# LayerNorm of a convolution branch: sums added first, the variance with tokens on partitions, the root on 128x4

## The reference

```python
def _layernorm(x, g, b):
    mu = jnp.mean(x32, axis=-1, keepdims=True)
    xc = x32 - mu
    y = xc * lax.rsqrt(jnp.mean(xc * xc, axis=-1, keepdims=True) + LN_EPS)
    return y * g + b

def _conv_module(u, ...):
    a, gt = u[..., :C_CONV], u[..., C_CONV:]
    h = a * jax.nn.sigmoid(gt)
    h = conv_general_dilated(h, conv_w, ...) + conv_b      # depthwise, width 31
    h = jax.nn.silu(_layernorm(h, ln_g, ln_b))
    return h @ w_pw_out
...
g = jax.nn.sigmoid(u_g + b_gate)
merged = g[..., :D] * y_conv + g[..., D:] * y_attn
```

## Time and profile before

| what | us |
|---|---|
| median of 3 runs | 3293.29 (3289.09 to 3296.37) |
| span of the profiled execution | 3293.2 |
| TensorE busy in it | 3180.6 |
| VectorE busy in it | 2023.7 |
| ScalarE busy in it | 1300.5 |
| GpSimd busy in it | 790.1 |

### The profile page before, as it was taken

How to read it: one execution, slowest core, us unless ns; L and a number is a source line. 1 busy time by engine, 2 the same in 40 slices (tenths; PEclk the granted TensorE clock), 3 DMA queues, 4 the chain that set the end, 5 groups by cost and what they waited for, 6 DMA issues and landing times.

```text
span 3293.2 us, 41912 instructions
## 1 busy us (share of the span) xinstructions
PE 3180.6 (97%) x15077; PEld 2620.5 (80%) x15077; DVE 2023.7 (61%) x3433; ACT 1300.5 (39%) x2213; POOL 790.1 (24%) x674
## 2 busy tenths in 40 slices
PE   8987999999999999999999999999999999999998
PEld 7865788788888888778887878876888888788886
DVE  6997357688807447599895862759667588510001
ACT  4336421533237431351112854228675168420111
POOL 3432200065775100011313520000212325101212
PEclk9998999999999999999999999999999999999999
DMA  7973856599893656535555046552555520445554
GB/s 236 302 242 128 307 188 208 185 292 289 290 298 122 243 202 216 195 139 194 192 192 185 14 182 226 206 180 90 217 192 193 201 74 20 173 166 193 194 196 165
DMA packets 178529, 635.97 MB, mean 193 GB/s; under 512 B 11358, under 2 KB 96906, under 8 KB 116777
## 3 DMA queue, kind: packets, MB, share of 16 engines
q1 hardware_dynamic: 164016, 583.05, 51.0%
q10 hardware_dynamic: 14328, 50.42, 3.9%
HBM read 474.04 MB, written 159.38 MB: 192 GB/s over the span
## 4 chain that ended last, share of the span: by engine, by line
PE 78%; ACT 5%; issue 3%; DVE 3%; DMA 1%; POOL 0%; ACTq 0%; DVEq 0%; POOLq 0%; SPq 0%
PE PS L1862 19%; PE PS L1813 15%; PE PS L1815 15%; PE PS L1814 15%; PE PS L2033 3%; PE PS L1836 2%; PE PS L1837 1%; PE PS L1838 1%; ACT TMP L903 1%; PE PS L2055 1%; PE PS L2056 1%; ACT probs L1028 1%; DVE W L1405 1%; PE PS L2086 1%; PE PS L2087 1%
## 5 line engine op out<-in xcount | busy, mean ns | idle before, releaser
L1862 PE MATMUL PS<-WS,HT 128*128 128x512 f32 x2088 | 482.7, 391 | 3.3 <-POOL WS L571 3.3
L1862 PEld LDWEIGHTS PS<-WS,HT 128*128 128x128 f32 x2088 | 393.9, 189 | 85.8 <-issue 3.7
L704 POOL TENSOR_TENSOR TMP<-TMP 128x512 f32<-128x512 f32 x88 | 114.5, 1302 | 1294.6 <-ACT TMP L1153 1294.6
L571 POOL TENSOR_TENSOR WS<-RAW,WS 128x1024 fp32r<-128x1024 f32 x116 | 279.9, 2413 | 569.1 <-ACT WS L776 556.3
L1813 PE MATMUL PS<-HF,WS 128*128 128x512 f32 x1024 | 398.7, 389 | 1.3 <-ACT TMP L903 0.9
L1815 PE MATMUL PS<-HF,WS 128*128 128x512 f32 x1024 | 398.4, 389 | 0.0
L1814 PE MATMUL PS<-HF,WS 128*128 128x512 f32 x1024 | 398.4, 389 | 0.0
L1422 DVE TENSOR_SCALAR_CACHE_REDUCE flags<-W,cand 128x640 uint8<-128x640 f32 (+9 forms) x272 | 372.6, 1370 | 35.6 <-DVE cand L1457 27.8
L1813 PE MATMUL PS<-HT,WS 128*128 128x512 f32 x816 | 322.2, 395 | 0.3 <-DVE HT L1242 0.3
L1815 PE MATMUL PS<-HT,WS 128*128 128x512 f32 x816 | 317.8, 389 | 0.0
L1814 PE MATMUL PS<-HT,WS 128*128 128x512 f32 x816 | 317.5, 389 | 0.0
(11 more groups left out here) (287 smaller groups left out, 6417.0 us busy)
## 6 DMA issues: line engine op xcount, KB each, us to landing
WS<-split_weights_scratch SPq DMA_DIRECT2D x234, 1024.0 KB, 4.8
split_weights_scratch<-WS SPq DMA_DIRECT2D x116, 1024.0 KB, 5.0
W<-split_weights_scratch SPq DMA_DIRECT2D x114, 1024.0 KB, 4.8
RAW<-in_w_in SPq DMA_DIRECT2D x34, 512.0 KB, 6.1
RAW<-in_w_ffn_gate SPq DMA_DIRECT2D x22, 512.0 KB, 6.3
RAW<-in_w_ffn_up SPq DMA_DIRECT2D x22, 512.0 KB, 6.4
RAW<-in_w_ffn_down SPq DMA_DIRECT2D x22, 512.0 KB, 5.7
gate_b_scratch<-TMP ACTq DMA_DIRECT2D x32, 256.0 KB, 5.3
```

What stands on the lines that cost most here:

```text
L571: nc.gpsimd.tensor_tensor(out=WS[:, slot, 1, :], in0=RAW[:, slot, :], in1=WS[:, slot, 0, :].bitcast(f32), op=ALU.subtract).then_inc(w_lo, 1)
L704: nc.gpsimd.tensor_tensor(out=TMP[:, s, :], in0=TMP[:, s, :], in1=TMP[:, 2 + s, :], op=ALU.mult).then_inc(h_prod, 1)
L1862: ins = mm(PS[:, 2 * t + half, :], lhs, split(c, w_part)[:, half * 512:(half + 1) * 512], start=first and part == 0 and w_part == 0, stop= ...
```

## The change

For groups 1 to 3, GpSimd and VectorE add the four chunks to one tile before the mean, so that TensorE needs one product for it. In all groups the squares are added to one tile, and the variance is four products with the summed squares as weights and one column of 1/512 moving, so that its result is 128 tokens on partitions by four columns. Epsilon, root, reciprocal and Newton step are done on 128x4. VectorE spreads the result to 128x512, four transposes bring it back to tokens along the free axis, and VectorE multiplies the chunks by it from PSUM. Mean, variance and transposes stand before gate chunks 5, 6 and 7 in every group; before, mean and variance stood before 5 and 6 in group 0 and before 4 and 5 in the others. The summed tiles lie in the convolution's input, which is read to its end by then.

```diff
-    LN_MEAN, LN_VAR = (5, 4, 4, 4), (6, 5, 5, 5)
+    LN_MEAN, LN_VAR = 5, 6
...
+        PAIRSUM = [GLU[:, c, 0:ROWS] for c in range(KC)]
...
+        tvar, trstd, tstep = (sb(name, [P, RT], f32) for name in ("token_var", "token_rstd", "token_step"))
...
@@ GpSimd, phase A
                     lo_run(c0, LEN[ph])
+                    if g > 0:
+                        pool.wait_ge(conv_step, KC * (TAPS * (g + 1) - 1) + 2)
+                        nc.gpsimd.tensor_tensor(out=PAIRSUM[0], in0=ACC[:, 0, :], in1=ACC[:, 1, :], op=ALU.add).then_inc(first_sum, 1)
+                        pool.wait_ge(sq_done, KC * g + 2)
+                        nc.gpsimd.tensor_tensor(out=PAIRSUM[1], in0=TMP[:, 0, :], in1=TMP[:, 1, :], op=ALU.add).then_inc(first_sum, 1)
...
@@ ScalarE
-                        if d == LN_MEAN[g] - 1:
+                        if d == LN_MEAN - 1:
...
-                        elif d == LN_VAR[g] - 1:
+                        elif d == LN_VAR - 1:
                             act.wait_ge(ln_sqrt, 2 * g + 1)
-                            nc.scalar.activation(TMP[:, 1, :], TMP[:, 0, :], ACT.Sqrt).then_inc(ln_sqrt, 1)
+                            nc.scalar.activation(trstd[:, :], tvar[:, :], ACT.Sqrt).then_inc(ln_sqrt, 1)
...
@@ VectorE
-                    nc.vector.memset(m8[:, :], 0.0).then_inc(acc_ready, 1)
                     if g == 0:
+                        nc.vector.memset(m8[:, :], 0.0).then_inc(acc_ready, 1)
                         search_turns(14, 18)
+                    else:
+                        chained(nc.vector.tensor_tensor(out=PAIRSUM[2], in0=ACC[:, 2, :], in1=ACC[:, 3, :], op=ALU.add))
+                        dve.wait_ge(first_sum, 2 * g - 1)
+                        nc.vector.tensor_tensor(out=PAIRSUM[2], in0=PAIRSUM[2], in1=PAIRSUM[0], op=ALU.add).then_inc(acc_ready, 1)
...
                     if g == 0:
+                        dve.wait_ge(sq_done, 2)
+                        chained(nc.vector.tensor_tensor(out=PAIRSUM[1], in0=TMP[:, 0, :], in1=TMP[:, 1, :], op=ALU.add))
+                    dve.wait_ge(sq_done, KC * g + KC)
+                    chained(nc.vector.tensor_tensor(out=PAIRSUM[3], in0=TMP[:, 2, :], in1=TMP[:, 3, :], op=ALU.add))
+                    if g > 0:
+                        dve.wait_ge(first_sum, 2 * g)
+                    nc.vector.tensor_tensor(out=PAIRSUM[3], in0=PAIRSUM[3], in1=PAIRSUM[1], op=ALU.add).then_inc(square_sum, 1)
+                    if g == 0:
                         search_turns(18, 20)
                     dve.wait_ge(var_psum, g + 1)
-                    nc.vector.tensor_scalar(TMP[:, 0, :], PS[:, 3, :], LN_EPS, None, ALU.add).then_inc(ln_sqrt, 1)
+                    nc.vector.tensor_scalar(tvar[:, :], PS[:, 3, 0:RT], LN_EPS, None, ALU.add).then_inc(ln_sqrt, 1)
...
-                    chained(nc.vector.reciprocal(y, y))
...
+                    chained(nc.vector.reciprocal(trstd[:, :], trstd[:, :]))
+                    chained(nc.vector.tensor_tensor(out=tstep[:, :], in0=trstd[:, :], in1=trstd[:, :], op=ALU.mult))
...
+                    nc.vector.tensor_copy(PAIRSUM[1].rearrange("p (t n) -> p t n", t=RT),
+                                          trstd[:, :].rearrange("p (t o) -> p t o", o=1).to_broadcast([P, RT, P])).then_inc(rstd_ready, 1)
+                    dve.wait_ge(rstd_psum, g + 1)
                     for c in range(KC):
-                        nc.vector.tensor_tensor(out=ACC[:, c, :], in0=ACC[:, c, :], in1=y, op=ALU.mult).then_inc(ln_ready, 1)
+                        nc.vector.tensor_tensor(out=ACC[:, c, :], in0=ACC[:, c, :], in1=PS[:, 3, :], op=ALU.mult).then_inc(ln_ready, 1)
...
@@ TensorE
-                            for c in range(KC):
-                                ins = mm(PS[:, 2, :], meanm[:, :], ACC[:, c, :], start=c == 0, stop=c == KC - 1)
+                            if g == 0:
+                                for c in range(KC):
+                                    ins = mm(PS[:, 2, :], meanm[:, :], ACC[:, c, :], start=c == 0, stop=c == KC - 1)
+                            else:
+                                ins = mm(PS[:, 2, :], meanm[:, :], PAIRSUM[2], start=True, stop=True)
...
-                        elif d == LN_VAR[g]:
-                            for c in range(KC):
-                                pe.wait_ge(sq_done, KC * g + c + 1)
-                                ins = mm(PS[:, 3, :], meanm[:, :], TMP[:, c, :], start=c == 0, stop=c == KC - 1)
+                        elif d == LN_VAR:
+                            pe.wait_ge(square_sum, g + 1)
+                            for t in range(RT):
+                                ins = mm(PS[:, 3, t:t + 1], PAIRSUM[3][:, t * P:(t + 1) * P], meanm[:, 0:1], start=True, stop=True)
                             ins.then_inc(var_psum, 1)
+                        elif d == LN_VAR + 1:
+                            pe.wait_ge(rstd_ready, g + 1)
+                            for t in range(RT):
+                                ins = nc.tensor.transpose(PS[:, 3, t * P:(t + 1) * P], PAIRSUM[1][:, t * P:(t + 1) * P], ident[:, :])
+                            ins.then_inc(rstd_psum, 1)
```

More of the change, by code:

```diff
@@ L296, in build_block @@
                                                                       sem("var_psum"), sem("ln_sqrt"), sem("ln_ready"))
+        first_sum, square_sum, rstd_ready, rstd_psum = sem("first_two_added"), sem("squares_added"), sem("token_rstd_ready"), sem("rstd_in_psum")
         xc_ready, sw_done, sw_hi, sw_ready = sem("xc_ready"), sem("sw_done"), sem("sw_hi"), sem("sw_ready")
@@ L1577, in _ @@
+                    if g == 0:
                         search_turns(18, 20)
                     dve.wait_ge(var_psum, g + 1)
-                    nc.vector.tensor_scalar(TMP[:, 0, :], PS[:, 3, :], LN_EPS, None, ALU.add).then_inc(ln_sqrt, 1)
+                    nc.vector.tensor_scalar(tvar[:, :], PS[:, 3, 0:RT], LN_EPS, None, ALU.add).then_inc(ln_sqrt, 1)
                     dve.wait_ge(ln_sqrt, 2 * g + 2)
-                    ms, y, t = TMP[:, 0, :], TMP[:, 1, :], TMP[:, 2, :]
-                    chained(nc.vector.reciprocal(y, y))
@@ new lines, in _ @@
+                    chained(nc.vector.tensor_tensor(out=tstep[:, :], in0=tstep[:, :], in1=tvar[:, :], op=ALU.mult))
+                    chained(nc.vector.tensor_scalar(tstep[:, :], tstep[:, :], -0.5, 1.5, ALU.mult, ALU.add))
+                    chained(nc.vector.tensor_tensor(out=trstd[:, :], in0=trstd[:, :], in1=tstep[:, :], op=ALU.mult))
+                    nc.vector.tensor_copy(PAIRSUM[1].rearrange("p (t n) -> p t n", t=RT),
+                                          trstd[:, :].rearrange("p (t o) -> p t o", o=1).to_broadcast([P, RT, P])).then_inc(rstd_ready, 1)
@@ L1988, in _ @@
                             pe.wait_ge(gate_free, KD * g + d - 1)
-                        if d == LN_MEAN[g]:
+                        if d == LN_MEAN:
                             pe.wait_ge(acc_ready, g + 1)
-                            for c in range(KC):
-                                ins = mm(PS[:, 2, :], meanm[:, :], ACC[:, c, :], start=c == 0, stop=c == KC - 1)
+                            if g == 0:
[3 more added lines that the diff above has]
+                                ins = mm(PS[:, 2, :], meanm[:, :], PAIRSUM[2], start=True, stop=True)
                             ins.then_inc(mean_psum, 1)
-                        elif d == LN_VAR[g]:
-                            for c in range(KC):
-                                pe.wait_ge(sq_done, KC * g + c + 1)
-                                ins = mm(PS[:, 3, :], meanm[:, :], TMP[:, c, :], start=c == 0, stop=c == KC - 1)
+                        elif d == LN_VAR:
+                            pe.wait_ge(square_sum, g + 1)
+                            for t in range(RT):
+                                ins = mm(PS[:, 3, t:t + 1], PAIRSUM[3][:, t * P:(t + 1) * P], meanm[:, 0:1], start=True, stop=True)
                             ins.then_inc(var_psum, 1)
+                        elif d == LN_VAR + 1:
[3 more added lines that the diff above has]
+                            ins.then_inc(rstd_psum, 1)
                         col_chunk(c0 + A_GA + d, d % 2, HT)
```

## The result

The changed kernel takes 3274.51 us (median of four runs, 3273.33 to 3275.36) beside 3294.83 for the kernel before on the same chip (3289.09 to 3297.58): a ratio of 0.9938, 95% interval 0.9925 to 0.995, faster by 20.3 us. The forecast was 3272.5, a saving of 20.7. The profiled execution has a span of 3272.0 us, and its own time is 1.8 us longer.

The account below looks back on a forecast made before the run. TensorE was taken to bound the kernel, busy 3180.6 of 3293.2 us. Savings of 17.9 us in groups 1 to 3 and 2.8 in group 0, 20.7 in all, gave 3272.5 us, range 3265 to 3283.

Parts of the forecast that it names:

- The mean: TensorE, groups 1 to 3: one product on a summed tile costs 0.98 us instead of 3.54.
- the wait of 0.99: TensorE's 0.99 us wait ahead of the mean in groups 1 to 3, forecast to go.
- The variance: TensorE, groups 1 to 3: four one-column products cost 1.02 us instead of 3.43, bounds 0.45 and 3.43.
- The sum of squares in time: Additions of squares end before TensorE's variance, covered by gate chunk 5: cost 0, without cover up to 1.3 us.
- The rival of late squares: GpSimd's or VectorE's addition is late; TensorE waits at the variance up to 1.3 a group: 3276.4 us, chance 0.12.
- Root and transposes at nothing: Root ready 2.3 us early under chunk 6, transposes fill the wait for swish: cost 0; 0.5 if swish were earlier.
- The rival of blocked small steps: VectorE's seven chained small steps could each wait for GpSimd, 2.08 us; all seven blocked give 3322 us; chance 0.05.
- Hidden anyway: Later groups' savings stop at index scores or attention; only group 0's 2.8 reaches the end: 3290.4 us, chance 0.08.
- Group 0: TensorE waits 4.45 us before the variance, yet VectorE's first gate product comes 2.8 us earlier, at 231.2; bounds 0 and 5.9.
- the half speed: After group 0's wait, TensorE runs 3.4 us at half clock, losing 1.7 us.
- The sum: 17.9 us from groups 1 to 3 (5.96 each) plus 2.8 from group 0: 20.7 us saved.
- The base: The profiled span of 3293.2 us, taken as the time before, with nothing of note around it.

Follow-up runs that it names:

- The third experiment: Changed kernel with the mean again four unsummed products in all groups, without the additions ahead of it: 3282.36 us, ratio 0.9963 to the kernel before.
- the first experiment: Kernel before, with mean and variance moved ahead of gate chunks 5 and 6 in all groups, nothing summed: 3291.93 us, ratio 0.9992.
- the second experiment: Changed kernel, sums kept, but variance one product and the root on 128x512 again, no transposes: 3277.14 us, ratio 0.9952 to the kernel before.
- the sixth experiment: Changed kernel with the four transposes issued twice: 3275.96 us, ratio 0.9946 to the kernel before.
- the later bits: Changed kernel with two instead of four of group 0's search bits ahead of the subtractions, run twice: 3268.37 and 3269.84 us.
- the ninth experiment: Changed kernel with the four variance products issued four times over, 32 records instead of 8: 3293.97 us, ratio 0.9998 to the kernel before.
- the fourth: Changed kernel with the squares unsummed, the variance 16 one-column products (32 records): 3290.62 us, ratio 0.9985 to the kernel before.
- the eighth: Changed kernel with two group 0 search bits moved later and group 0's squares unsummed (32 records there): 3271.47 us, ratio 0.9932 to the kernel before.

## Why the prediction was right, step by step

**The mean** was sized at 0.98 and measures 0.89; the wait of 0.99 before it is gone. The third experiment prices its six records at 2.56 a group, and the first shows that moving mean and variance without the sums takes only 0.37 off, because 0.7 of the wait comes back behind the wide root.

**The variance** was the unknown: its bounds were 0.45 and 3.43, the value taken 1.02, the measured one 0.92. The eight records run at the pace of the transposes, 0.10 to 0.11 each, at full clock in groups 1 to 3. The Trainium skill (TensorE: Matmul & The Clock Gate, LDWEIGHTS) gives 107 ns for a load however few columns move; the 3.49 us for 32 records agree with that.

**The sum of squares in time**: 0.68 to spare where 0.5 was worked out. The rival of late squares did not come about: GpSimd's addition ended at 1337.88 and VectorE's, which started at 1337.72, took 0.70, so nothing lengthened it there. The two ran side by side for 0.16 us at most, so the 2.77 of the earlier trace rows was not put to the test in this stage; it came back in group 0 of the second experiment (2.76).

**Root and transposes at nothing**: the root is there 2.5 us early (2.3 forecast), and the sixth experiment shows the transposes hidden even when doubled. The rival of blocked small steps is out: each took 0.16 to 0.18 us, and the spreading 0.43.

**Hidden anyway** is out as well: what the three groups gained in their stages reached the end, but for the shifts of the clock between them.

**Group 0** had the right mechanism with one term too small. Forecast were a wait of 4.45, 3.4 us at half clock, and 2.8 us saved at the first gate product. In the three executions of the changed kernel that product came at 232.36, 232.57 and 230.85, against 234.07 in the earlier trace rows, but VectorE's subtractions start at 207.60, 207.64 and 205.60 in them, so the last owes 2.0 us to what went before. Counted from the subtractions (207.40 in the earlier trace rows, as the forecast counts it), 1.9, 1.8 and 1.4 are saved; the waits ahead of the variance were 5.20, 5.07 and 3.69. The term that was mis-sized is the half speed. In the first trace it lasted from the restart at 212.41 to 218.07, 5.7 us and not 3.4: from the variance to the transposes are 9.10 us there and 6.38 in group 2, so it cost 2.7 instead of 1.7, and the first gate product came 1.1 later than forecast. With the later bits and a wait of 0.94 or 1.36 the clock stays up, and from the subtractions to the gate product are 23.00 and 22.57 us instead of 24.76 to 25.25. That the search then ended 2.25 earlier, and not 1.7, came from the search itself: from the first gate product to its end are 27.97 us instead of 28.51, which nothing had forecast.

**The sum** came out at 20.7 in part by luck: the steps of groups 1 to 3 were 0.2 a group too small, 0.6 in all, and that of group 0 was 0.6 too large at the end of the search. The shifts between the stages (0.3, -1.4, -1.7, 3.4) were not in it; they are larger than the steps' errors and nearly cancel. The base was short as well. The prediction took the span of 3293.2 for the time and let nothing lie around it, but executions of the kernel before are 2.2 us longer than their spans (3295.61 beside 3293.4 in the first experiment), and its medians were 3294.83 to 3295.82. So the saving, 20.3, was met more closely than the 3272.5.

## What to carry to other kernels

When TensorE sets the end, adding tiles on engines with time to spare before a product with constant weights takes whole products off the path; here that was 2.56 us of the 6.15 a group for the mean alone. Price such additions by who comes next on the engine that makes them: in groups 1 to 3 a whole gate chunk covered them, in group 0 the same additions stood behind search bits and left TensorE waiting, and searching two of the bits later was worth another 3 to 6 us by the medians, 2.1 to 3.4 of it seen at the end of the search. A stage that looks the same in every group must be costed once for each group whose neighbours differ.

## What the hardware showed that was not expected

TensorE's granted clock fell behind a run of products that had no gap. With 32 records of one moving column, 0.11 us each, TensorE was busy 3.40 of 3.40 us at 1.00 (2.4 GHz), and the next 3.80 us were granted 0.56 on average, with products 0.43 apart, 1.2 GHz (the ninth experiment, and alike in the fourth and the eighth). With eight such records the clock stayed at 1.00, in groups 1 to 3 of every kernel that has them. A full busy share of TensorE in the profile did not keep the clock up here, so a stretch has to be read by its granted clock and by what was issued in it. Nothing between eight and 32 records was run. The fall cost as much as the records: 24 more of them took 2.6 us a group, the half speed behind them another 1.6 to 3.3.
